# Two-group streaming encoder step: the key columns of the attention latents first, and the first head pair staged in another order

## The reference, cut to what matters

```python
z = hn @ w_in                                   # (544, 1024) @ (1024, 384 + 256 + 32)
c_q, c_kv, k_pe = z[..., :384], z[..., 384:640], z[..., 640:]
q = (rms(c_q, g_q) @ w_qup).reshape(b, l, 16, 96)
q = rms(cat([q[..., :64], rope(q[..., 64:])]), g_qn)
latent, k_pe = rms(c_kv, g_kv), rope(k_pe)      # both are outputs too
kv = (cat([cached_latent, latent]) @ w_kvup).reshape(b, l, 16, 64 + 64)
k = rms(cat([kv[..., :64], broadcast(k_pe)]), g_kn);  v = kv[..., 64:]
o = softmax(q @ k.T * 96**-0.5, chunk-causal mask) @ v
```

## Time and profile before

| | |
|---|---|
| median of 3 runs | 2466.8 us (2465.01 to 2467.2) |
| the profiled execution | 2467.75 us |
| its span, first to last instruction | 2465.9 us |
| PE busy | 2274.8 us (92%) |
| DVE, ACT, POOL busy | 1715.8, 1075.7, 324.1 us |
| mean granted TensorE clock | 0.953 |

### The profile page before, as it was taken

One profiled execution on the slowest core, in us unless ns is written; L12 is line 12 of the kernel. 1 busy time (PEld: TensorE's weight loads), 2 busy tenths in 40 slices (PEclk: granted clock), 3 DMA queues, 4 the chain that ended last, 5 costly groups with the idle time before them and its releaser, 6 DMA issues. The chain is left out here.

```text
span 2465.9 us, 45118 instructions
## 1 busy us (share of the span) xinstructions
PE 2274.8 (92%) x16514; PEld 2183.8 (89%) x16514; DVE 1715.8 (70%) x2706; ACT 1075.7 (44%) x1799; POOL 324.1 (13%) x284
## 2 busy tenths in 40 slices
PE   4999999688988999999999999999978888999997
PEld 4999999677877999999987999999867778999997
DVE  8976974457666698498445995895366648975973
ACT  5532542355555454154323552453246545532541
POOL 1000001134333100000113000001143311000001
PEclk9999999788889999999999999999978889999998
DMA  2222232000000222222223222222121112222221
GB/s 106 102 88 92 102 103 73 24 19 19 9 10 27 79 101 98 81 103 102 73 68 115 104 107 89 87 107 83 66 52 45 45 35 77 102 98 82 102 105 60
DMA packets 72810, 187.55 MB, mean 76 GB/s; under 512 B 40720, under 2 KB 42288, under 8 KB 61440
## 3 DMA queue, kind: packets, MB, share of 16 engines
q1 hardware_dynamic: 71424, 181.67, 21.6%
q0 software_dynamic: 1280, 4.49, 0.5%
HBM read 178.79 MB, written 7.35 MB: 75 GB/s over the span
## 5 line engine op out<-in xcount | busy, mean ns | idle before, releaser
L565 PE MATMUL ps<-xs_hi,w_hi 128*128 128x272 f32 x1408 | 410.3, 291 | 49.8 <-DVE w_lo_more L1538 28.3
L567 PE MATMUL ps<-xs_hi,w_lo 128*128 128x272 f32 x1408 | 408.0, 290 | 0.0
L566 PE MATMUL ps<-xs_lo,w_hi 128*128 128x272 f32 x1408 | 407.2, 289 | 0.0
L1043 ACT ACTIVATE w_hi<-raw 128x1408 fp32r<-128x1408 f32 (+3 forms) x124 | 146.0, 1183 | 506.4 <-PE ps L590 246.0
L1072 ACT ACTIVATE w_hi<-w_blocks 128x1024 fp32r<-128x1024 f32 x176 | 186.8, 1061 | 323.1 <-PE ps L567 159.1
L565 PEld LDWEIGHTS ps<-xs_hi,w_hi 128*128 128x128 f32 x1408 | 266.5, 189 | 53.6 <-issue 29.7
L565 PE MATMUL ps<-xs_hi,w_hi_more 128*128 128x272 f32 x1056 | 306.5, 290 | 2.4 <-ACT scratch L1118 1.8
L566 PE MATMUL ps<-xs_lo,w_hi_more 128*128 128x272 f32 x1056 | 305.9, 290 | 0.0
L590 PE MATMUL ps<-hid_hi,w_hi 128*128 128x272 f32 x1312 | 273.3, 290 | 9.1 <-DVE w_lo L1508 5.5
L590 PE MATMUL ps<-hid_lo,w_hi 128*128 128x272 f32 x1312 | 271.8, 289 | 0.0
L590 PE MATMUL ps<-hid_hi,w_lo 128*128 128x272 f32 x1312 | 271.8, 288 | 0.0
(11 more groups left out here) (257 smaller groups left out, 5165.2 us busy)
## 6 DMA issues: line engine op xcount, KB each, us to landing
w_blocks<-w_ffn_in SPq DMA_DIRECT2D x88, 1024.0 KB, 4.8
raw<-w_ffn_out SPq DMA_DIRECT2D x64, 704.0 KB, 4.1
raw<-w_b_kv SPq DMA_DIRECT2D x16, 512.0 KB, 3.3
raw<-w_a_out SPq DMA_DIRECT2D x8, 512.0 KB, 3.2
raw<-w_b_q SPq DMA_DIRECT2D x8, 512.0 KB, 3.3
raw<-w_b_out SPq DMA_DIRECT2D x8, 512.0 KB, 3.3
raw<-w_a_in SPq DMA_DIRECT2D x4, 672.0 KB, 4.0
raw<-w_a_qup SPq DMA_DIRECT2D x8, 288.0 KB, 2.7
```

Of the source, the lines that this page charges most:

```text
L565: pe.matmul(out, lhs[0], rhs[0], start=start, stop=False, skip_group_check=more)
L566: pe.matmul(out, lhs[0], rhs[1], start=False, stop=False, skip_group_check=more)
L567: return pe.matmul(out, lhs[1], rhs[0], start=False, stop=stop, skip_group_check=more)
L1043: act.activation(wh[par][:, 0:n], raw[par][:, 0:n], ACT.Copy).then_inc(w_hi, 1)
```

## The change

1. The columns of `w_a_in` are reordered on the host: c_kv and k_pe come first (columns 0 to 287), c_q behind them (288 to 671). So c_kv and k_pe are complete after Z1.
2. ACT squares c_kv and takes its root, and DVE turns k_pe, scales c_kv and splits it, while PE does Z2 and Z3. PE transposes the key latents between the second and third token tile of Z3. Each token tile of Z3 is signalled by itself (d0 to d3). The cached latents are copied and split before Z2's weights.
3. `lat` moves from `arena` into the hidden activations' buffer, so that pair 0's keys can be written while c_q is still in use. Pair 0's value weights (unit M+1) are split into free columns of slot 0 (`w_first`).
4. PE does pair 0's first two key groups, the query latents' transposes, the other three key groups, then the queries.
5. Pair 0's norms: ACT takes a root and DVE a reciprocal, in place of POOL's power; DVE scales the queries in place of POOL. The order of the transposes is keys, cached keys, queries, sample (`turn_first`, with banks of its own).
6. The scores start when q0 and p0 are split; pair 1's queries are projected in two parts between the score blocks, pair 1's keys after them. Pair 1's `square_keys`, `mean_square_keys` and the splits of pair 2's weights move into `first_head(0)`.

`PROJ`, `STAGE` are cut in two each (`PROJQ`/`PROJK`, `STAGEQ`/`STAGE`), which renames semaphores. The second attention keeps its order.

```diff
@@ PE: key latents inside Z3, then the prologue
-            pe.wait_ge(*st["dve"].at("lat4"))
...
+            def z_done(t, mm):
+                mm.then_inc(Z["st"]["pe"].sem, 1)
+                if t == 1:
+                    pe.wait_ge(*Z["st"]["dve"].at("lat4"))
+                    turn_latents(0, LC, LAT_BANKS)
...
-                    pe.wait_ge(*Z["st"]["dve"].at("u4"))
-                    project_q(0, first[0], [])
-                    project_kv(0, first[0], [])
-                turn_staged(0, first[1], first[0])
-                for u in range(5):
-                    scores(0, u, 0)
-                if mla:
-                    project_q(1, first[1], first[0])
-                    project_kv(1, first[1], first[0])
-                if mla:
-                    pe.wait_ge(*prj["act"].at("v4", 1))
+                    pe.wait_ge(*Z["st"]["dve"].at("ks1"))
+                    project_kv(0, first[0], [], range(2), w_first)
+                    pe.wait_ge(*Z["st"]["dve"].at("cq4"))
+                    turn_latents(Q_OFF, QC, Q_BANKS)
+                    project_kv(0, first[0], [], range(2, 5), w_first)
+                    pe.wait_ge(*Z["st"]["dve"].at("qs2"))
+                    project_q(0, first[0], [])
+                    turn_first(first[1], first[0])
+                    for u in range(3):
+                        scores(0, u, 0, True)
+                    project_q(1, first[1], first[0], range(1))
+                    scores(0, 3, 0, True)
+                    project_q(1, first[1], first[0], range(1, 3))
+                    scores(0, 4, 0, True)
+                    project_kv(1, first[1], first[0])
+                    pe.wait_ge(*prk["act"].at("v4", 1))
@@ ACT: latents
...
+                if m == 2:
+                    square_latents("sk", 0, KV_RANK, ST_MS + 5)
...
+            act.activation(w_first[0], raw[1][:, 0:LC * 4 * DV], ACT.Copy).then_inc(w_hi, 1)
+            latents_hi("k", LC, latT[0], KEYS, SEQ + PAST, LAT_BANKS, None)
+            square_latents("sq", Q_OFF, Q_RANK, ST_MS)
@@ ACT: pair 0
+                    project(0, False, range(2), True)
+                    latents_hi("q", QC, cqT[0], T, SEQ, Q_BANKS, G_AQ)
+                    project(0, False, range(2, 5), True)
+                    square_keys(0)
+                    act.wait_ge(*prk["dve"].at("ssk2", 0))
+                    first_root(10, 28)
+                    stage_values(0, False)
+                    act.wait_ge(w_used, U + 1 + PRIME + 1)
+                    split_hi(0, U + 2, U // 2 + 2, QC * 2 * DA)
+                    square_queries(0)
+                    stage_part("p0", 0, True)
+                    act.wait_ge(*prq["dve"].at("ssq", 0))
+                    first_root(0, 10)
+                    stage_part("p1", 0, True)
+                    stage_part("c0", 0, True)
+                    stage_part("q0", 0, True)
+                    stage_part("c1", 0, True)
+                    stage_part("q1", 0, True)
+                    exp(0, 0, 0)
+                    stage_samples(0)
+                    exp(0, 1, 0)
+                    split_hi(1, U + 3, U // 2 + 2, LC * 4 * DV)
+                    for u in range(2, 5):
+                        exp(0, u, 0)
+                    project(1, True, range(2), True)
+                    square_queries(1)
+                    project(1, True, range(2, 5))
@@ DVE: latents
+            ahead(U + 3)
+            latent_rstd("k", ST_MS + 15)
...
+            ahead(U + 4)
...
+            latents_lo("k", LC, latT, KEYS, SEQ + PAST, LAT_BANKS, None)
...
+            latent_rstd("q", ST_MS + 10)
...
+            latents_lo("q", QC, cqT, T, SEQ, Q_BANKS, G_AQ)
@@ DVE: pair 0
+                    sum_keys(0)
+                    take_q(0, range(1), True)
+                    dve.wait_ge(*L["first"]["act"].at("sdk"))
+                    dve.reciprocal(stat[:, ST_R + 10:ST_R + 28], stat[:, ST_VAR + 10:ST_VAR + 28]
+                                   ).then_inc(prk["dve"].sem, 1)
+                    norm_keys(0, True)
+                    take_q(0, range(1, 3), True)
+                    rope_queries(0, 0)
+                    split_lo(0, U + 2, QC * 2 * DA)
+                    sum_queries(0)
+                    dve.wait_ge(*L["first"]["act"].at("sdq"))
...
+                    stage_part("p0", 0, True)
+                    stage_part("q0", 0, True)
+                    stage_part("p1", 0, True)
+                    top(0, 0, 0)
+                    stage_part("c0", 0, True)
+                    top(0, 1, 0)
+                    stage_part("c1", 0, True)
+                    inverse_sum(0, 0, 0)
+                    top(0, 2, 0)
+                    stage_part("q1", 0, True)
+                    stage_samples(0)
+                    inverse_sum(0, 1, 0)
+                    take_q(1, range(1))
+                    split_lo(1, U + 3, LC * 4 * DV)
+                    top(0, 3, 0)
+                    inverse_sum(0, 2, 0)
+                    take_q(1, range(1, 3))
+                    rope_queries(1, 0)
+                    top(0, 4, 0)
+                    inverse_sum(0, 3, 0)
+                    inverse_sum(0, 4, 0)
+                    sum_queries(1)
...
@@ DVE: first_head(p, before)
+                        if j == 1 and mla and not before:
+                            mean_square_keys(1)
                     top(1, 4, p)
+                    if mla and not before:
+                        split_units(2)
@@ POOL
+                    pool.wait_ge(*prk["dve"].at("ms", 0))
+                    shared_keys(0)
+                    stage_values(0, False)
+                    normalise(0, 0)
+                    project_at(1)
```

More of the change, by code:

```diff
@@ L44 @@
 LC = KV_RANK // P
+R_OFF, Q_OFF = KV_RANK, KV_RANK + ROPE
 EPS = 1e-6
@@ L285, in build @@
         pS = rstd[:, 0:2 * PT_S].rearrange("p (g w) -> p g w", g=2)
-        lat = arena[:, 0:NT * ZW].rearrange("p (t w) -> p t w", t=NT)
+        lat = at_col("latent", C_HID[0], NT * ZW)[:, :].rearrange("p (t w) -> p t w", t=NT)
+        w_first = [t[0][:, QC * 2 * DA:QC * 2 * DA + LC * 4 * DV] for t in (wh, wl)]
         o = NT * ZW
@@ L718, in tok_unit @@
                         bank_free(c, t)
-                    out = ps[:, TOK_BANKS[(NT * c + t) % 7], 0:n]
+                    out = ps[:, TOK_BANKS[(NT * c + t) % 7] if banks is None else banks[NT * c + t], 0:n]
                     for k in range(kn):
@@ L786, in bank_of, with project_q @@
                     return b
-                def project_q(it, uses, before):
+                def project_q(it, uses, before, groups=range(3)):
                     unit_ready(M["u"] + 2 * it)
-                    for n in range(3):
+                    for n in groups:
                         b = bank_of(f"q{n}", uses, before)
@@ new lines, in latent_rstd, with latents_lo @@
+            def latent_rstd(name, col):
+                dve.wait_ge(*st["act"].at(f"sd{name}"))
+                dve.reciprocal(stat[:, col + 10:col + 15], stat[:, col:col + 5]).then_inc(inc, 1)
+                dve.wait_ge(*st["dve"].at(f"r{name}"))
+            def latents_lo(name, n, dst, length, o_s, banks, scale):
+                for j in range(2 * n):
+                    jj = j % n
+                    dve.wait_ge(*st["act"].at(f"{name}{j}" if j < n else f"{name}s{n - 1}"))
+                    src = ps[:, banks[j], :] if j < n else ps[:, banks[n], jj * DEC:(jj + 1) * DEC]
+                    o = jj * length + (0 if j < n else o_s)
+                    c = slice(o, o + (SEQ if j < n else DEC))
+                    low(dst[1][:, c], src, dst[0][:, c], None if scale is None else gc[:, scale + jj:scale + jj + 1], inc)
@@ new lines, in _ @@
+            ahead(U + 1)
+            inverse(Z["rms"])
+            dve.wait_ge(*st["act"].at("cache"))
+            both = [a[:, :].rearrange("p (j w) -> p j w", j=LC)[:, :, SEQ:SEQ + PAST] for a in latT]
+            low(both[1], cached_raw.rearrange("p (j w) -> p j w", j=LC), both[0], None, inc)
+            ahead(U + 2)
+            rms_tok(st)
+            dve.wait_ge(w_used, U + 1 + PRIME + 1)
+            for t in range(NT):
+                take_z(0, t)
+            turn_shared()
+            ahead(U + 3)
@@ L1819, in split_p, with take_q @@
                     low(pT[1][:, o:o + w], src[:, c:c + w], pT[0][:, o:o + w], None, ainc)
-                def take_q(it):
-                    for n in range(3):
+                def take_q(it, groups=range(3), first=False):
+                    for n in groups:
                         if n == 0:
@@ new lines, in stage_part @@
+                def stage_part(name, it, first=False):
+                    out, n, o, g = {"q": (qT, T, 0, g_q), "p": (kT, KEYS, 0, g_k), "c": (kT, KEYS, SEQ, g_k)}[name[0]]
+                    st, hh = stq if name[0] == "q" else stg, int(name[1])
+                    b = (FIRST_BANKS if first else banks).get("t" + name, banks["t" + name])
+                    dve.wait_ge(*st["act"].at(name, it))
```

(16 more changed lines are left out.)

492 lines of the change are left out of this document (263 added, 229 removed), and 3 rows, old and new, of the table STAGE.

## The result

The changed kernel takes 2445.6 us (median of 4 runs, 2441.57 to 2447.0) where the kernel before takes 2466.4 beside it (4 runs, 2465.01 to 2467.2): a ratio of 0.9913, with a 95% interval of 0.9901 to 0.9926. It is faster by 20.8 us. 2438.5 was forecast, with a range of 2432 to 2446. The sign and the place are right, the time lies at the very end of the range, and a quarter of the forecast gain of 28.25 is missing. In all 14 runs of the changed kernel made for this study the time lies between 2441.6 and 2449.0, so 2438.5 is outside what it does.

What follows compares the result with a forecast made beforehand. PE was taken as idle behind a serial chain of small DVE, ACT and POOL steps before pair 0's scores. 29.0 us earlier at first_head(0) less 0.75 gives 28.25: 2467.75 to 2439.5, median about 2438.5, range 2432 to 2446.

Steps and rivals of the forecast that it cites:

- Part 1, the latents: Z2 and Z3: c_kv scaled at about 437.4, no wait inside Z3, added transposes lengthen Z3 by 1.2 us.
- The 5 us of cover: In Z3: c_kv is ready at about 437.4, PE needs it at 442.7, so PE does not wait.
- slower than before: Rival: c_kv not scaled when PE asks mid-Z3; needs 29 us of wait to end slower; chance 0.025.
- Parts 2 and 3, the norms: From Z3's end at 449.6 through pair 0's norms and transposes: first score at 473.8, 24.0 us earlier.
- Part 4, the clock: Scores and pair 1's products: clock falls near 469, returns at 479.5; first_head(0) at 492.3, 29.0 us earlier.
- the one row at 474: Kernel before, query products: clock returned within the microsecond from 474, 5.7 us after products began at 468.4.
- Its bounds, −1.5 to +8 us: Range allowed for the clock's effect on first_head(0)'s start, from warm throughout (490.8) to cold throughout (about 500).
- Part 5, what is given back: In first_head(0), moved DVE steps delay pair 1's key transposes to 14.9 us after its start, against 14.15: 0.75 lost.
- the clock stays low: Rival: low clock from 469 until the loop, costing 7.7 us more; gain 20.6, time 2446.2; chance 0.08.
- longer norm chain: Rival: wait before key or query transposes 3 to 5 us longer; gain 24, time 2443; chance 0.13.
- The clock never falls: Rival: clock stays up, gain 28.25 + 1.5, up to 33; 2434 to 2437 us; chance 0.13 (or more gain).

Runs made afterwards that it cites:

- after, second: The changed kernel again, no edit, timed beside the first group: 2445.0 us, ratio 0.9922.
- after, third: The changed kernel again, no edit, timed beside the third group: 2446.2 us, ratio 0.9912.
- filled: Changed kernel plus 18 unread 512-column products in TensorE's wait for the queries' scaling of pair 0: 2440.0 us, ratio 0.9896.
- splits moved: Changed kernel with the splits of pair 2's weights moved from first_head(0) to ahead of it: 2439.4 us, ratio 0.9905.
- both: Changed kernel with the 18 fill products and the earlier splits of pair 2's weights, timed twice: 2431.1 us (0.9865) and 2435.6 us (0.9867).
- the latents alone: Only the new latent order on the kernel before, pair 0, pair 1 and first_head as before: 2455.5 us, ratio 0.9958.
- the kernel with the power again: Changed kernel with pair 0's norms by POOL's power and its queries scaled by POOL again: 2449.9 us, ratio 0.9936.
- the simpler order: Changed kernel with fill products, earlier splits and all five score blocks of pair 0 before pair 1's projections: 2436.6 us, ratio 0.9873.

## Why the prediction was right, and where it was off

The span can be cut at three starts that every trace has: the first score, `first_head(0)`, and pair 2's power on POOL (560.56 in the kernel before). For the two stages between them the table gives the length and the mean granted clock, both from the windows; what a stage lost by the clock is its length times what the clock lacks to 1 (an upper value, as a low clock over an idle PE costs nothing).

| trace | first score | first_head(0) | stage 1: us, clock | stage 2: us, clock | rest | span |
|---|---|---|---|---|---|---|
| before | 497.80 | 521.30 | 23.50, 0.70 | 39.26, 0.91 | 1905.3 | 2465.9 |
| after | 473.85 | 494.50 | 20.65, 0.71 | 43.16, 0.88 | 1902.1 | 2439.8 |
| after, second | 473.78 | 497.26 | 23.48, 0.62 | 40.20, 0.87 | 1904.8 | 2442.3 |
| after, third | 474.55 | 492.78 | 18.23, 0.81 | 41.87, 0.84 | 1910.0 | 2444.6 |
| filled | 473.36 | 495.04 | 21.68, 0.69 | 40.30, 0.87 | 1901.6 | 2436.9 |
| splits moved | 474.33 | 495.58 | 21.25, 0.69 | 38.30, 0.91 | 1900.8 | 2434.7 |
| both | 473.36 | 488.65 | 15.29, 1.00 | 37.94, 0.96 | 1902.2 | 2428.8 |
| both, second | 473.45 | 488.71 | 15.26, 1.00 | 38.42, 0.91 | 1907.5 | 2434.6 |

**Part 1, the latents: right.** c_kv done at 436.7 (437.4 forecast), no wait inside Z3, the transposes 1.3 us, and the latents alone give 10 us. The 5 us of cover, on which the rival *slower than before* hung, were 5.6.

**Parts 2 and 3, the norms: right as a chain, and to 0.05 us by luck.** The first score was put at 473.8 and came at 473.85, 473.78 and 474.55. Inside that sum two errors of a microsecond cancel. The wait for the shared key part is 0.84 and not 1.9, because DVE's adding of the k_pe sums took 0.18 us instead of 0.6 and the chain was a microsecond ahead. The rope's step then cost 1.1 us more beside POOL, so the queries' transposes began at 471.15, where 471.2 was forecast; the wait before them is 4.48 and not 3.2, as the key transposes were done sooner. The collision between POOL and DVE was foreseen at the right place, 2.22 us, and missed at two more: the rope (1.40 for 0.31), and pair 2's splits in `first_head(0)` (2.33 for two, 1.4 forecast). The rule cited in the prediction from the Trainium skill, SBUF — State Buffer, "Who interferes with whom", names all three: operations of DVE with two inputs in SBUF beside one of GpSimd that reads it.

**Part 4, the clock: this is the step that failed.** It said that the clock returns "some 5.7 us after 473.8, at 479.5". The place of the fall was right to 2 us (468.7, and 471.2 and 471.1 in the other two). The return came at 485.8, 491.7 and 481.3. The work in between was priced well: at full clock stage 1 takes 15.3 us, in both profiles of the two edits together. Add half of the low time and the changed kernel's rows follow: 473.85 + 15.3 + 6.0 = 495.1 for 494.50, 473.78 + 15.3 + 9.0 = 498.1 for 497.26, 474.55 + 15.3 + 3.4 = 493.3 for 492.78. With 5.7 us low it would be 492.0, and the forecast was 492.3. So the mis-sized term is the return of the clock, 5.7 from the one row at 474, where it measured 6.8, 11.9 and 17.9. Its bounds, −1.5 to +8 us, held: the three starts lie 0.5, 2.2 and 5.0 behind the forecast one. But both bounds were too narrow by the prediction's own prices. At full clock throughout, three score blocks and 13 products would be 1.45 and 1.35 us less, so −2.8 and not −1.5; measured, 15.3 us from 473.8 on gives 489.1, which is −3.2. Cold throughout, the 86 products left at 479.5 alone cost 9 us more, and not 7.7; by the measured stage, of which PE is busy 14.7 us, it would be some 504 instead of 500 (an estimate: 473.8 + 15.3 + 14.7). The trace of before held a warning. Its 6.2 us of scores did not bring the clock back, as the prediction says itself; it came back at 511.7, 4.5 us into the products that began at 507.2 behind an idle 3.2 us, and 13.9 us after the first score. The sum counted its 5.7 us from the first score all the same, as if scores were such products. That alone isn't the whole miss: in the second trace 18 us of scores and products at a busy share of 0.98 weren't enough.

**Part 5, what is given back: the term itself right, another missing.** The key transposes start 14.46, 14.47 and 14.71 us after `first_head(0)`, against 14.15 before: 0.3 to 0.6 given back, 0.75 forecast. (That start is set by DVE's chain; a low clock ahead of it only shortens PE's wait.) But stage 2 as a whole takes 43.2, 40.2 and 41.9 us against 39.3, which is 2.5 more in the mean. The clock accounts for most of it: length times what it lacks to 1 is 5.2, 5.2 and 6.7 us, in the mean 5.7, against 3.5 before. In the profile shown it falls once there, behind the wait for pair 1's key scaling (509.3 to 519.9). In the second it falls at 505.3, 512.1 and 532.6, in the third at 498.4 and 508.6, each time both ahead of that wait and behind it; in the kernel before it was low for 3.4 us twice. So the wait of 4.28 us goes with one fall of several, and none of them was a term of the sum. With the splits moved, the stage takes 38.3, 37.9 and 38.4 us and loses 3.4, 1.5 and 3.5.

**The rest of the program** takes 1901 to 1910 us in all eight rows, the kernel before in their middle. The prediction's "beyond that the loop over pairs is as before" holds on the whole, but this term scatters by 9 us. It goes with the clock that each execution got: the four rows of 1901 to 1902 us have a mean clock of 0.96 there, the four of 1905 to 1910 have 0.95. In the three traces of the changed kernel it scatters more (7.8 us) than either stage (5.3 and 3.0).

**The sum.** The three spans of the changed kernel are 26.1, 23.6 and 21.3 us under that of the kernel before. In the mean: 26.45 at `first_head(0)`, less 2.5 given back, less 0.3 in the rest, makes 23.7. By medians of runs the gain is 20.8, as the one profile of the kernel before is 1.4 us above the median of its four runs and the three profiles after are 1.5 below theirs in the mean. The forecast was 28.25: 2.6 of what is missing were lost at `first_head(0)`, 1.7 behind it, and some 3 are the rest and the distance of the profiled executions from the medians. Of the 21 us the latents alone give 10, and the norms 5 (by the kernel with the power again). No run takes alone what makes up the other 6: the key products that now stand in the wait, the new order of pair 0's transposes, and what both do to the clock.

**The rivals.** The size that came, 20.8 by the medians and 23.7 in the profiles, lies at the border of what was given 0.08 as *the clock stays low* and of what was given 0.13 as a *longer norm chain*. No longer chain is there. The mechanism is that of *the clock stays low*, a part of the way: it stayed low for 7 to 18 us of dense products, though not until the loop in every case. The rule cited there from the Trainium skill, TensorE: Matmul & The Clock Gate, "HAM oscillation", was taken not to reach a dense run; the first score to 491.7 at 0.50 is one, so the argument "54 dense products follow, and such a run did bring it back" was too strong. It isn't that rule's case either, as PE had no waits there. *The clock never falls* was seen up to `first_head(0)` with the two edits together: gains of 34.3 and 30.7 us by the medians, against a forecast of 28.25 + 1.5 to 33. The sum has no term of its own for the interleaving; by the traces it is worth 1.7 us with the clock up and nothing that shows with the clock low.

**What stays open.** Why the clock fell at 475.7 in the filled kernel and not in three traces of the same PE instructions up to that place isn't settled, and neither is what sets the time of its return between 6.8 and 17.9 us. PE's instructions up to there don't decide it; what does was not found. That the moved splits help beyond the filling is likely (11 to 14 us for both, 5 for the filling), but the kernel with both has been set beside the changed kernel only once, and never beside the filled one.

## What to carry to other kernels

A chain of small steps in front of the tensor engine can be drawn from single rows to a microsecond or so for each of its parts, and closer only if every collision between GpSimd and two-input operations of VectorE is drawn too. The clock can't: give its return a range as wide as all stretches of the trace show it, not the value of the friendliest one, and price a bound with the same care as the forecast. Look also at what the change makes late behind the place you work on: the low stretches there cost 2 us more than before. When a prologue has such waits, filling them and moving optional work out of the next chain can be worth half as much again as the reordering itself (11 to 14 us on top of 21 here). A single profiled execution isn't enough to say so: the first score scatters by 0.8 us between three executions of the changed kernel, `first_head(0)` by 4.5 and the end of the span by 4.8. And a time that shows no difference doesn't show that a step is worth nothing: the interleaving's 1.7 us could be read from the trace alone.

## What the runs showed of the hardware

- The granted clock can fall with PE nearly always busy. In the filled kernel it left 2.4 GHz within the microsecond from 475 (0.87), PE busy 0.98 us of it, with no idle longer than 0.9 us since 463.9; in three other profiles of the same PE instructions up to there (both edits twice, and with the simpler order) it stayed.
- Dense work doesn't bring it back at a fixed time: 6.8, 11.9 and 17.9 us after the first score in three executions of one program, with PE busy without a break.
- A DVE operation with two inputs in SBUF (128x160) took 0.31 us alone and 1.40 beside a GpSimd one begun 0.31 us earlier.
- A GpSimd power of 18 columns took 3.22 to 3.23 us and one of 10 columns 1.96; ACT's root and DVE's reciprocal of the same columns 0.31 + 0.26 and 0.30 + 0.22.
- Executions of one kernel differ by 7 us (2441.6 to 2449.0), and on the whole the longer ones have the lower mean clock: 0.960 for 2441.57 and 0.954 for 2447.0 in the changed kernel, though 0.955 for 2449.02.
